# Last RMSNorm of a two-layer backbone on one core: column sums and transposes replaced by a product with a matrix of ones, root and reciprocal on 640 columns

## The reference

```python
def _rms_norm(x, g):
    xf = x.astype(jnp.float32)
    y = xf * lax.rsqrt(jnp.mean(xf * xf, axis=-1, keepdims=True) + EPS)
    return (y * g.astype(jnp.float32)).astype(x.dtype)

x = x + g2 * (jnp.square(jax.nn.relu(h2 @ lp['w_ff1'])) @ lp['w_ff2'])   # end of each layer
y_prompt = _rms_norm(xp, final_norm_g)      # (1, 128, 1024)
y_sample = _rms_norm(xs, final_norm_g)      # (1, 512, 1024)
```

## Time and profile before

| | value |
|---|---|
| median of 3 runs | 1854.69 us (1854.47 to 1855.54) |
| profiled execution, its own time | 1854.28 us |
| span in the profile, first to last instruction | 1852.5 us |
| mean granted TensorE clock | 0.982 |
| PE busy | 1760.6 us, 95% of the span |
| DVE busy | 1253.1 us, 68% |
| ACT busy | 858.1 us, 46% |
| POOL busy | 494.9 us, 27% |

### The profile page before, as it was taken

One profiled execution on the slowest core, in us unless ns is written; L12 is line 12 of the kernel. 1 busy time (PEld: TensorE's weight loads), 2 busy tenths in 40 slices (PEclk: granted clock), 3 DMA queues, 4 the chain that ended last, 5 costly groups with the idle time before them and its releaser, 6 DMA issues.

```text
span 1852.5 us, 33404 instructions
## 1 busy us (share of the span) xinstructions
PE 1760.6 (95%) x13514; PEld 1667.4 (90%) x13514; DVE 1253.1 (68%) x2063; ACT 858.1 (46%) x1479; POOL 494.9 (27%) x404
## 2 busy tenths in 40 slices
PE   4999998998999999999999999898989999999997
PEld 2899986688999999999999999666989999999997
DVE  2688684577734677676665567555877777788886
ACT  1455337643342231321325543574435666666663
POOL 4000011064342150421451000203443232332235
PEclk7999999999999999999999999999999999999998
DMA  8652231021367879688527862202422677877662
GB/s 344 254 200 84 76 102 31 1 64 64 138 232 211 295 230 328 236 272 286 183 83 204 187 148 88 68 1 65 91 87 86 206 245 246 296 273 259 216 215 86
DMA packets 117158, 314.04 MB, mean 170 GB/s; under 512 B 27269, under 2 KB 53677, under 8 KB 97293
## 3 DMA queue, kind: packets, MB, share of 16 engines
q1 hardware_dynamic: 110860, 276.87, 42.1%
q0 software_dynamic: 4608, 33.56, 9.4%
q10 hardware_dynamic: 1536, 1.48, 0.2%
HBM read 284.70 MB, written 94.18 MB: 205 GB/s over the span
## 4 chain that ended last, share of the span: by engine, by line
PE 83%; DVE 8%; issue 3%; ACT 3%; DMA 2%; SPq 0%; ACTq 0%; POOL 0%; POOLq 0%; DVEq 0%
PE PS L2237 46%; PE PS L2306 18%; PE PS L2511 2%; DMA ADA<-ada 2%; PE PS L2602 1%; PE PS L2539 1%; PE PS L2701 1%; PE PS L2560 1%; PE PS L2673 1%; PE PS L2615 1%; PE PS L2528 1%; DVE MPR L1721 1%; PE PS L2709 1%; PE PS L2374 1%; PE PS L2462 1%
## 5 line engine op out<-in xcount | busy, mean ns | idle before, releaser
L2237 PE MATMUL PS<-HH,HI 128*128 128x320 f32 (+1 forms) x1280 | 299.4, 315 | 4.5 <-DVE HL L1470 4.5
L2237 PE MATMUL PS<-HL,HI 128*128 128x320 f32 (+1 forms) x1280 | 294.9, 312 | 0.0
L2237 PE MATMUL PS<-HH,LO 128*128 128x320 f32 (+1 forms) x1280 | 293.3, 310 | 0.0
L929 ACT CAST HI<-RAW 128x2048 fp32r<-128x2048 f32 x64 | 121.8, 1904 | 273.1 <-PE PS L2237 246.2
L2237 PEld LDWEIGHTS PS<-HH,HI 128*128 128x128 f32 x1280 | 215.1, 190 | 5.1 <-issue 5.0
L2237 PEld LDWEIGHTS PS<-HL,HI 128*128 128x128 f32 x1280 | 218.8, 191 | 0.0
L2237 PEld LDWEIGHTS PS<-HH,LO 128*128 128x128 f32 x1280 | 216.7, 190 | 0.0
L2306 PE MATMUL PS<-FB,WHL 128*128 128x320 f32 x1344 | 199.6, 309 | 6.3 <-DVE TMP L1598 3.2
L2306 PEld LDWEIGHTS PS<-FB,WHL 128*128 128x128 f32 x1344 | 197.1, 188 | 8.7 <-DVE WHL L1515 6.4
L2306 PE MATMUL PS<-HB,WHL 128*128 128x322 f32 (+1 forms) x1344 | 201.5, 312 | 2.4 <-DVE TMP L1598 1.4
L2306 PEld LDWEIGHTS PS<-HB,WHL 128*128 128x128 f32 x1344 | 200.4, 190 | 3.1 <-issue 3.1
(11 more groups left out here) (343 smaller groups left out, 2895.8 us busy)
## 6 DMA issues: line engine op xcount, KB each, us to landing
RAW<-ws SPq DMA_DIRECT2D x64, 1024.0 KB, 5.1
wp<-ws SPq DMA_DIRECT2D x32, 1024.0 KB, 8.2
RAWB<-wp SPq DMA_DIRECT2D x128, 256.0 KB, 4.0
WM<-adt SPq DMA_DIRECT2D x48, 512.0 KB, 9.1
RAWB<-ws SPq DMA_DIRECT2D x96, 256.0 KB, 3.4
FS<-hb SPq DMA_DIRECT2D x28, 640.0 KB, 8.0
ADA<-ada SPq DMA_DIRECT2D x16, 1024.0 KB, 7.7
wp<-ws POOLq DMA_DIRECT2D x16, 1024.0 KB, 10.2
```

What stands on the lines that cost most here:

```text
L929: nc.scalar.copy(HI[g % 2][:, :], RAW[g % 2][:, :]).then_inc(hi_ready, 1)
L2237: last = pe.matmul(bank(2 * u + a)[:, 0:e], w[:, cols], m[:, a * HT:a * HT + e], start=(k == 0 and f), stop=(k == KT - 1 and e_))
```

## The change

The sums of the last norm are formed by products whose stationary operand is a 128x128 matrix of ones (`ones`) and whose moving operand is a half of the tile of squares, 320 columns wide. Each output column then holds the sum on all 128 partitions at once, in banks 4 and 5. ACT takes the root of all 640 columns into `RB`, DVE takes the reciprocal of `RB` in place, and then copies it into `pair(3)` for its own six multiplications. POOL reads `RB` after the reciprocal. The second PSUM copy, both turns and ACT's copy are gone. `FIRST_OUT` names the 6 that stood there as a number.

```diff
                 for k in range(KT):
-                    sp.wait_ge(y_rb[k >= 6], k + 1 if k < 6 else k - 5)
+                    sp.wait_ge(y_rb[k >= FIRST_OUT], k + 1 if k < FIRST_OUT else k + 1 - FIRST_OUT)
...
                 act.wait_ge(nss, 5)
-                nc.scalar.activation(RT[:, 0:NB], bank(4)[:, 0:NB], ACT.Sqrt, bias=eps, scale=1.0 / D).then_inc(nrt, 1)
-                act.wait_ge(nrb, 6)
-                nc.scalar.copy(flat(RB[:, :, :]), pair(3)).then_inc(nrd, 1)
+                nc.scalar.activation(RB[:, :, :], even(2), ACT.Sqrt, bias=eps, scale=1.0 / D).then_inc(nrt, 1)
...
                 dve.wait_ge(nrt, 5)
-                nc.vector.reciprocal(RT[:, 0:NB], RT[:, 0:NB]).then_inc(nrr, 1)
-                dve.wait_ge(nrb, 5)
-                for k in range(6):
+                nc.vector.reciprocal(RB[:, :, :], RB[:, :, :]).then_inc(nrd, 1)
+                dve.wait_ge(nrd, 5)
+                nc.vector.tensor_copy(pair(3), flat(RB[:, :, :])).then_inc(nrr, 1)
+                dve.wait_ge(nrr, 5)
+                for k in range(FIRST_OUT):
                     dve.wait_ge(y_fg, k + 1)
                     y = flat(YF[:, k, :, :])
-                    nc.vector.tensor_tensor(y, y, pair(2), ALU.mult).then_inc(y_rb[0], 1)
+                    nc.vector.tensor_tensor(y, y, pair(3), ALU.mult).then_inc(y_rb[0], 1)
...
                 pe.wait_ge(nsq, squared(4) + 11)
-                column_sums(SQA, True, False)
+                def sums_everywhere(x, first, final):
+
+                    for a in range(2):
+                        last = pe.matmul(bank(4 + a)[:, 0:HT], ones, x[:, a * HT:(a + 1) * HT], start=first, stop=final)
+                    return last
+                sums_everywhere(SQA, True, False)
                 pe.wait_ge(F["lsq"], fast_base(DEPTH - 1)["lsq"] + 2)
-                column_sums(SQ7, False, False)
+                sums_everywhere(SQ7, False, False)
                 pe.wait_ge(F["lsq"], fast_base(DEPTH - 1)["lsq"] + 3)
-                last = column_sums(SQX, False, True)
-                last.then_inc(nss, 1)
-                norm_turn(4)
-                norm_turn(4, 3)
+                sums_everywhere(SQX, False, True).then_inc(nss, 1)
```

More of the change, by code:

```diff
@@ L489, in build @@
         pro_buf = [4, 5, 6, 7, 8, 0, 1, 2]
+        FIRST_OUT = 6
         blocks = [[LB if s == LB else (s if d == 0 else LB - 1 - s) for d in range(2)] for s in range(NB)]
@@ L917, in _ @@
                 pool.wait_ge(nrd, 5)
-                for k in range(6, KT):
+                for k in range(FIRST_OUT, KT):
                     pool.wait_ge(y_fg, k + 1)
```

## The result

The median of the changed kernel is 1858.24 us over 19 runs, beside 1854.02 us over 19 runs of the kernel before. The ratio is 1.0017, 95% interval 1.0009 to 1.0025, so it is 1.7 to 4.6 us slower, with 3.1 in the middle. The two medians lie 4.2 us apart, which is also inside this interval. The forecast was 1857.3 us, or +2.6, no change that matters, on its slow side, with a range of 1855.7 to 1859.0. Ratios leave out runs at a lower granted clock, here two of rsqrt_on_act that took 2191 and 2900 us at 0.744 and 0.559, for a reason that no run shows. Single runs of either kernel spread over 5 to 8 us, so what one step costs is read from the tail of a profile and not from a time.

A forecast was written before the change was run, and what follows sets the result against it. A one-engine-at-a-time chain, then transfers at full bandwidth, bound the tail, its end fixed 9.30 us behind the first multiplication. −1.37 + 0.52 + 4.01 − 1.42 + 0.88 = +2.62 us on 1854.69 gave 1857.3, range 1855.7 to 1859.0.

The forecast's parts named there:

- The reciprocal: DVE's reciprocal on 640 columns instead of 5: 4.20 us less today's 0.19, +4.01 us, with everything behind it waiting.
- 8 ns a column: Rival: DVE's wide reciprocal costs more per column, 5.2 us in all, sum +3.6, time 1858.3; chance 0.07.
- a copy's pace: Rival: DVE's wide reciprocal takes only 0.82 us, sum −0.8, time 1853.9; chance 0.03.
- Root: ACT's root on 640 columns out of PSUM instead of 5: 0.79 us against 0.27, +0.52 us.
- Copy: DVE's copy of 640 columns to PSUM ahead of its multiplications: 0.82 us and 0.03 on either side, +0.88 us.
- Outputs: Multiplications and transfers unchanged: end stays 9.30 us behind the first multiplication, and POOL's earlier factors buy nothing.
- the rival in which the tail shortens: With POOL's tiles ready early, issue rather than bandwidth sets the end; 0.5 to 1.5 us back, time 1856.3; chance 0.07.
- Turn: PE's five transposes between the reciprocal's end and DVE's first multiplication leave the path: −1.42 us.
- Sums: PE's wide column sums at full clock let the root start at 1839.92 instead of 1841.29: −1.37 us.
- ACT's last two gains are level with the sums: Ahead of the root, ACT's gains, formerly hidden under PE, end at 1839.79, level with PE's sums.
- narrow products had let the clock fall: In PE's sums: narrow products, not idle time, preceded the clock's fall to 0.50; wide ones should hold it up.
- the clock falls all the same: Rival: clock drops during the changed kernel's sums; sums +0.2 instead of −1.37, total +4.2 us, 1858.9; chance 0.13.

The follow-up runs named there:

- rsqrt_on_act: Changed kernel with ACT's reciprocal root of the 640 sums replacing root, DVE's reciprocal and copy, table loaded early; ratio to the kernel before 0.9985 (0.9975 to 0.9994).
- half_recip: Changed kernel with the reciprocal on 320 of the 640 columns, so half the output is scaled wrongly; ratio to the kernel before 1.0011 (1.0000 to 1.0023).
- half_out: Changed kernel with each output transfer carrying only 320 of 640 columns; tail 16.0 us from the first record of tile 3's sums, instead of 17.6.
- before_again: Second profile of the unedited kernel before; tail 13.5 us from the first record of SQ's sums, where the first profile had 15.15.
- before_third: Third profile of the unedited kernel before; tail 13.0 us from the first record of SQ's sums, where the first profile had 15.15.
- before_fourth: Fourth profile of the unedited kernel before; tail 13.6 us from the first record of SQ's sums, where the first profile had 15.15.
- filler: Kernel before with an unread 512-column float32 product on PE between the sums of SQA and SQ; tail 14.15 us from ACT's square of tile 3.
- narrow_two: Changed kernel with the first two tiles of squares summed by narrow products into an unread bank; tail 17.65 us from the first record of tile 3's sums.
- no_copy: Changed kernel without the copy to PSUM, DVE's multiplications reading the factors from SBUF; ratio to the kernel before 1.0035 (1.0021 to 1.0049).
- no_copy_alone: On top of no_copy, DVE multiplies all eight tiles from SBUF with POOL idle; ratio to the kernel before 1.0008 (0.9998 to 1.0018).

## Why the prediction was right, and where it was not

*The reciprocal* (+4.01 forecast) is the change: 4.15 us less 0.19, +3.96. half_recip shows that it scales by the column and lies on the path. The 6.25 ns for each column lie between the two slopes of the forecast, 6.1 and 6.5. The rivals with 8 ns a column and with a copy's pace (0.82 us) fell.
*Root* (+0.52) measured 0.79 − 0.27 = +0.52. *Copy* (+0.88) measured 0.83 with 0.04 ahead of it and 0.03 behind, +0.90. *Outputs*: the end is 9.2 to 9.3 us behind the first multiplication in both kernels, in half_recip and in rsqrt_on_act, and half_out shows that bandwidth holds it there. POOL's earlier start bought nothing, and the rival in which the tail shortens fell.

*Turn* (−1.42): from the reciprocal's end to the first multiplication it took 1.32 us in before_again, 0.85 in before_third and 1.42 in before_fourth, depending on where in it the clock fell. So −1.42 is the upper end of what goes.

*Sums* (−1.37) is the step that failed, by its size and by its reason. I took SQX's ten records in 2.27 us as the price of narrow sums. That was the price of the early fall. At a granted clock of 1.00 the ten take 1.25 us and the four wide ones that replace them 1.24, so the two ways of summing cost the same. The earlier trace rows already said so: `SQA`'s ten took 1.17, and I forecast 1.2 for its four. The root starts at +2.42 or +2.43 in three of four profiles of the kernel before, beside +2.46 and +2.45 in the changed one, so the wide products gained nothing there.

ACT's last two gains are level with the sums, as forecast, but the root follows PE: it starts 0.03 or 0.04 us behind the end of PE's last sum in every profile shown here (1841.25 and 1841.29 in the first, 1841.19 and 1841.23 in before_again, 1838.45 and 1838.48 in the changed kernel, 1840.77 and 1840.81 in filler). In before_again it even starts before the record of the gains ends, at 1841.25. In filler the gains end 0.13 before the root.

My argument that narrow products had let the clock fall drew on two places with a fall and one without. narrow_two and the three repeats had narrow products and the full clock until the last sum. The first trace also held a fall that speaks against it. This one, at 1291.8 us, came behind a stretch in which PE was busy for 0.99 of 3.4 us, with eight records of 128 columns and none of one:

```profile
1288.40:1291.80 3.40, 0.99 (x8) 0.81 (x9) 2.89 (x5) 0.59 (x1) 2.22 (x3) 1.00 0.66 135
1291.90:1295.20 3.30, 3.30 (x45) 3.01 (x44) 0.29 (x1) 1.76 (x5) 2.18 (x3) 0.50 0.00 0
```

That wide products hold the clock up isn't refuted, since all eight profiles with wide sums, in every tile or in the last alone, kept it at 1.00 until the last sum. It isn't shown either, since three of the four profiles of the kernel before did the same.

With these corrections the step-by-step account against before_again is +0.04 (sums), +0.52, +3.96, −1.32, +0.90 and −0.02 (tail), +4.1 us, and 17.6 − 13.5 is 4.1. Against the mean of the four profiles of before, 13.8, it is +3.8, inside the measured +1.7 to +4.6. The forecast of +2.6 was inside as well, but in part by luck: it came from an execution in which the kernel before had lost about 1.5 us that it lost in none of the three repeats, and the interval, 3 us wide, doesn't tell +2.6 from +4.0, which is what the sum gives with nothing for the sums. Two rivals came closer to the median of 1858.24, the 8 ns a column (1858.3) and the early fall in the changed kernel (1858.9), and neither of their mechanisms is in the profiles. The forecast's own range of 1856.7 to 1858.0 is also wider than its bounds, which add up to about 1856.9 to 1857.5. The other versions fit the same mean: half_recip 15.6 − 13.8 = +1.8 (measured +2.0), no_copy +5.4 (measured +6.5, interval 3.9 to 9.1), no_copy_alone +2.9 (measured +1.5, −0.4 to 3.3, near the upper end), rsqrt_on_act −1.3 (measured −2.8, −4.6 to −1.1).

The rival "the clock falls all the same" looked for the risk in the wrong kernel. What mattered wasn't that the changed kernel might lose the clock, but that the kernel before keeps it through the sums in three of four profiles.

## What to carry to other kernels

Work on few columns and then spread the result, unless the operation is as cheap per column as a copy: a reciprocal on 640 columns, the same on every partition, cost 4.15 us, where one of 5 columns and a turn through PE cost 0.2 and 0.9 to 1.4. Compare two ways of doing a step at the same granted clock before pricing the gain: here ten narrow records took 1.25 us and four wide ones 1.24. Before a term of 1 us is read from one profile, look whether it hangs on the granted clock, and take a second profile if it can be had.

## What was unexpected of the hardware

- DVE and POOL, both with all operands in SBUF: six multiplications of 640 columns took 7.17 us instead of 4.47 and POOL's two 4.19 instead of 3.04. With DVE alone eight took 5.97. DVE's loss sat in single multiplications, up to 2.15 us beside a median of 0.82.
- The moment at which the granted clock falls in the same tail moved between 0.6 and 3.6 us behind the same instruction over four profiles of the same kernel, and the tail with it from 15.15 to 13.0 us.
- With a dummy activation of one column ahead of a wait, ACT's table load (1.28 us) lay off the path, and neither the squares and gains nor the reciprocal root behind it loaded a table again. A version without the dummy wasn't run.
